# Splitting the first weight tile of five projection stages inside the stage in front of each

## The chip, the cores and the metric

One core of a Trainium2 chip runs the whole kernel in one launch. The metric is the device time of that core in microseconds (us), lower is better. The engines are TensorE (PE, with its weight loads shown as PEld), VectorE (DVE), ScalarE (ACT), GpSimd (POOL) and SyncE (SP), which issues nearly all DMA transfers.

## The reference

A first block (one layer) and a second block (two layers) work on 512 tokens of 2048 features; the second block also carries 256 context tokens. All of it is fp32.

```python
# first block
proj = rmsnorm(x) @ w_in                       # 2048 x 5120
y_s = s5_scan(u_s, ...); y_s = gelu(y_s)
y_s = y_s * sigmoid(y_s @ w_glu + b_glu) * silu(g_s)
y_d = diff_attention(q, k, v, ...) * silu(g_d)
y_x = memory_attention(q_x, rmsnorm(mem) @ w_mem_kv) * silu(g_x)
x = x + rmsnorm(concat([y_s, y_d, y_x]) @ w_out)
# second block, for l in 0, 1
h = rmsnorm_2(x) * (1 + scale) + shift         # from silu(c) @ ada_w[l]
q, k, v, up, uf, g = split_proj(h @ w_in[l])   # 2048 x 4608; context tokens too
att = latent_attention(rope(norm(q)), rope(norm(k)), v, kc, vc)
mixed = concat([att, multiscale_pool(up), fourier_mix(uf)])
x = x + gate * ((mixed * silu(g)) @ w_out[l])
# at the end rmsnorm_2(x)
```

## The kernel before

**How a weighted product is done.** Every large product is fp32 made of three fp32r products. The activations lie in SBUF as a high and a low part, `h_hi` and `h_lo`, features on partitions, tokens along the row (512, or 768 with context). A weight tile is 128 output columns by all 2048 inputs, 1 MB, and is used as 16 blocks of 128x128. It is loaded by SP into one of four slots of `raw`, ScalarE rounds it into `w_hi` (2 slots), VectorE writes `w_lo = raw - w_hi` (2 slots), and TensorE runs `w_hi*h_hi`, `w_hi*h_lo`, `w_lo*h_hi` over the 16 blocks into a PSUM bank. The counters (semaphores) are `raw_full[0..3]`, `hi_done`, `lo_done` and `w_used`. ScalarE may write `w_hi` of tile n when TensorE is through tile n-2 (`w_used.at(n - 1)`).

**The helper `linear`** (lines 220 to 412) runs one such product: a loop over tiles on each engine. On ScalarE tile n is split (line 319), then the result of tile n-1 is read out, then comes side work. VectorE does the same with line 348 for the split. TensorE waits for `lo_done.at(n + 1)` and runs lines 389 to 391. With `ahead` the two engines split the first tile of the following stage before the last result is read (lines 324 to 328 and 355 to 357), and with `primed` the four slots of `raw` were loaded by the stage in front.

**The stages in order.** `opening`, `ssm_and_conditions` (32 tiles of `w_in`, the state-space scan on VectorE and GpSimd, and the conditions from `ada_w`), a `linear` of 8 tiles of `w_mem` (the memory's keys and values, 256 tokens, with the preparation of the GLU as side work: class `GluPrepare`), `glu` (4 double tiles), `middle_attention` (16 units of differential and 16 of memory attention), `out_projection` with `w_out`, and then twice `projections(l)` (36 tiles), `layer_attention(l)` and `out_projection(w_out2, ...)` (16 tiles, through `linear`), and `final_norm`. Each stage is a block of the language: its engines start together once all five are through the stage in front, SP's last waits among them. Inside a block every engine runs its own list in the order written, and waits only on semaphores.

**Where the first split stands now.** In five stages it is the first instruction of ScalarE and of VectorE: the memory product (lines 319 and 348 of its first turn), `glu` (`split(0)`, lines 1272 and 1302), and the three calls of `out_projection` (lines 319 and 348). In the other stages with such products it is already done in the stage in front (`ahead`).

**What is around it.** At the end of `ssm_and_conditions` ScalarE copies the last result of the conditions (`ada_copy`, 957), the last projection result (`out_`, 947) and the last scan output (`y_copy`, 952); VectorE ends its scan at line 1051 and adds the conditions (1004). SP loads the four tiles of `w_mem` at line 893. In the memory product the side work of a turn is, on VectorE, lines 1177, 1182, 1186, 1188 and 1192, and on ScalarE lines 1164, 1166 and 1170; after the eighth turn three more turns of side work alone (`rest`) close the stage. In `middle_attention` ScalarE and VectorE run a loop over units g: read-out (1849), exponential (1823), gate (1842) and results on one, maximum (1909, 1911), weights (1925, 1927), gates (1941) and results (1946, 1953) on the other; each waits for the other in every unit. The last GpSimd instruction of the stage is line 1797. In `projections` the last turns (`kind == "mix"`, c = 0 to 9) also run the pooling and Fourier branches, and read-out of tile n is a tanh on ScalarE (2365) and a product on VectorE (`gate_out`, 2502). SP's turn c = 9 stores the last mixed rows (`store_mixed(3)`) and loads the first head (2320). `layer_attention` has SP load head 0's gate and mixed row, then call `prime` (line 414: four tiles of `w_out2`), and then load head 1's queries (1387).

```python
# before, linear, ScalarE: the split, then the read-out of the tile in front
for j in range(4):
    n = 4 * i + j
    act.wait_ge(raw_full[j].h, raw_full[j].at(16 * (i + 1)))
    act.wait_ge(w_used.h, w_used.at((n - 1) * per_slot))
    act.activation(w_hi[:, j % 2, 0:size], raw[:, j, 0:size], ACT.Copy).then_inc(hi_done.h, 1)
```

## Time and profile before

| | |
|---|---|
| median of 3 runs | 3012.83 us (3012.28 to 3015.34) |
| profiled execution | 3011.3 us |
| its span, first to last instruction | 3009.5 us |
| PE busy, share of span | 2825.9 us, 94% |
| DVE, ACT, POOL busy | 1517.9, 987.8, 503.3 us |
| mean granted TensorE clock | 0.973 of full speed |

```profile
PE   7899999988769999999999999899989999989897
PEld 5666665667447868888888877688878877867785
DVE  6587887867563552125533436423253385546334
ACT  4444444434353333122211126411142232226321
POOL 2544445424341030000000002100010000002000
PEclk9999999999789999999999999999999999999998
```

Each column is a fortieth of the span (75 us), each digit the busy share in tenths, and PEclk the granted TensorE clock in tenths. TensorE is nearly always busy; the columns with 6 to 8 are the attention stages and the ends of stages. The memory product, `glu`, `middle_attention` and the first `out_projection` lie in columns 9 to 14, the attention of layer 0 in columns 24 to 26, that of layer 1 in columns 36 and 37.

### The profile page before, as it was taken

The page shows a single profiled execution, that of the slowest core. Times are in us where ns is not written, and L with a number is a line of the kernel's source. Part 1 is how long each engine was busy: PE and PEld are TensorE (multiplying, and loading weights), DVE is VectorE, ACT ScalarE, POOL GpSimd, SP SyncE. Part 2 cuts the span into 40 slices and gives each one's busy share as a digit, 9 for nine tenths or more (in the row PEclk, how much of TensorE's full clock was granted, in tenths as well). Part 3 has the DMA queues.
Part 4 walks back from the last instruction along what each step waited for, and adds up shares of the span by engine and source line. Part 5 has one row for each costly group of instructions (what it writes and reads, how often), then busy time and mean ns, then how long its engine had stood idle before and what let it go on. Part 6 is the DMA issues. An engine that isn't in the chain of part 4 may idle for free. (4 is left out here: it accounts for less than half of the span.)

```text
span 3009.5 us, 36233 instructions
## 1 busy us (share of the span) xinstructions
PE 2825.9 (94%) x14018; PEld 2228.0 (74%) x14018; DVE 1517.9 (50%) x2057; ACT 987.8 (33%) x1708; POOL 503.3 (17%) x607
## 2 busy tenths in 40 slices
PE   7899999988769999999999999899989999989897
PEld 5666665667447868888888877688878877867785
DVE  6587887867563552125533436423253385546334
ACT  4444444434353333122211126411142232226321
POOL 2544445424341030000000002100010000002000
PEclk9999999999789999999999999999999999999998
DMA  5577787765213242233333341322313444441421
GB/s 189 183 306 304 286 313 290 282 248 175 101 57 126 86 180 83 78 110 134 117 108 131 121 159 64 116 78 96 119 49 107 143 168 147 154 163 60 161 98 56
DMA packets 111687, 447.20 MB, mean 149 GB/s; under 512 B 11440, under 2 KB 19760, under 8 KB 76208
## 3 DMA queue, kind: packets, MB, share of 16 engines
q1 hardware_dynamic: 111536, 445.16, 40.7%
q8 instruction: 98, 1.61, 0.2%
q14 instruction: 53, 0.43, 0.0%
HBM read 375.25 MB, written 69.86 MB: 148 GB/s over the span
## 5 line engine op out<-in xcount | busy, mean ns | idle before, releaser
L2732 PE MATMUL ps<-h_hi,w_hi 128*128 128x512 f32 x1600 | 576.9, 361 | 0.0
L2733 PE MATMUL ps<-h_lo,w_hi 128*128 128x512 f32 x1600 | 565.1, 353 | 0.0
L2734 PE MATMUL ps<-h_hi,w_lo 128*128 128x512 f32 x1600 | 561.4, 351 | 0.0
L389 PE MATMUL ps<-h_hi,w_hi 128*128 128x512 f32 (+1 forms) x1152 | 413.1, 359 | 35.0 <-DVE w_lo L348 35.0
L390 PE MATMUL ps<-h_lo,w_hi 128*128 128x512 f32 (+1 forms) x1152 | 412.1, 358 | 0.0
L391 PE MATMUL ps<-h_hi,w_lo 128*128 128x512 f32 (+1 forms) x1152 | 410.0, 356 | 0.0
L2732 PEld LDWEIGHTS ps<-h_hi,w_hi 128*128 128x128 f32 x1600 | 301.9, 189 | 49.8 <-issue 6.2
L2733 PEld LDWEIGHTS ps<-h_lo,w_hi 128*128 128x128 f32 x1600 | 301.7, 189 | 46.5 <-issue 6.2
L2734 PEld LDWEIGHTS ps<-h_hi,w_lo 128*128 128x128 f32 x1600 | 300.8, 188 | 43.7
L2510 DVE TENSOR_TENSOR w_lo<-raw,w_hi 128x2048 fp32r<-128x2048 f32 x64 | 146.4, 2287 | 310.7 <-ACT w_hi L2413 310.6
L389 PEld LDWEIGHTS ps<-h_hi,w_hi 128*128 128x128 f32 x1152 | 220.0, 191 | 70.1 <-DVE w_lo L348 37.9
L391 PEld LDWEIGHTS ps<-h_hi,w_lo 128*128 128x128 f32 x1152 | 219.2, 190 | 31.9
L390 PEld LDWEIGHTS ps<-h_lo,w_hi 128*128 128x128 f32 x1152 | 219.8, 191 | 30.5
L2366 ACT ACTIVATE xw<-ps 128x512 f32<-128x512 f32 x88 | 42.2, 517 | 593.4 <-PE ps L2734 552.9
L1465 POOL TENSOR_TENSOR h_lo<-xw,h_hi 128x768 fp32r<-128x768 f32 (+1 forms) x16 | 25.4, 1588 | 1237.1 <-ACT h_hi L1513 1237.1
L1111 PE MATMUL ps<-h_hi,w_hi 128*128 128x512 f32 x512 | 203.5, 397 | 12.9 <-DVE w_lo L1020 6.9
L1112 PE MATMUL ps<-h_lo,w_hi 128*128 128x512 f32 x512 | 200.2, 391 | 0.0
L1113 PE MATMUL ps<-h_hi,w_lo 128*128 128x512 f32 x512 | 200.2, 391 | 0.0
L2092 ACT ACTIVATE wide<-xw 128x512 f32<-128x512 f32 (+3 forms) x48 | 33.8, 703 | 486.9 <-DVE stat L2116 373.8
L348 DVE TENSOR_TENSOR w_lo<-raw,w_hi 128x2048 fp32r<-128x2048 f32 x56 | 128.7, 2303 | 87.6 <-ACT w_hi L319 87.6
L2108 DVE SCALAR_TENSOR_TENSOR xw<-ps,mods,xw 128x512 f32 (+3 forms) x48 | 31.8, 662 | 258.9 <-PE ps L391 244.7
L1111 PEld LDWEIGHTS ps<-h_hi,w_hi 128*128 128x128 f32 x512 | 96.6, 189 | 55.7 <-DVE w_lo L1020 21.2
(385 smaller groups left out, 4729.5 us busy)
## 6 DMA issues: line engine op xcount, KB each, us to landing
raw<-w_in SPq DMA_DIRECT2D x112, 1024.0 KB, 5.2
raw<-ada_w SPq DMA_DIRECT2D x96, 1024.0 KB, 8.3
raw<-w_out SPq DMA_DIRECT2D x48, 1024.0 KB, 4.9
proj<-xw SPq DMA_DIRECT2D x60, 384.0 KB, 2.6
xw<-proj SPq DMA_DIRECT2D x72, 256.0 KB, 3.4
xw<-proj SPq DMA_DIRECT2D x46, 384.0 KB, 3.4
xw<-resid SPq DMA_DIRECT2D x8, 1536.0 KB, 11.7
proj<-wide SPq DMA_DIRECT2D x32, 256.0 KB, 10.8
```

The source lines that it names most:

```text
L348: dve.tensor_tensor(w_lo[:, j % 2, 0:size], raw[:, j, 0:size], w_hi[:, j % 2, 0:size].bitcast(F32), ALU.subtract).then_inc(lo_done.h, 1)
L389: pe.matmul(a_[q], wh, h_hi[:, h0 + k, lo:hi], start=k == 0, stop=False)
L390: pe.matmul(a_[q], wh, h_lo[:, h0 + k, lo:hi], start=False, stop=False)
L391: ins = pe.matmul(a_[q], wl, h_hi[:, h0 + k, lo:hi], start=False, stop=k == nk - 1)
L1111: pe.matmul(acc, wh, h_hi[:, k, 0:T], start=k == 0, stop=False)
L1112: pe.matmul(acc, wh, h_lo[:, k, 0:T], start=False, stop=False)
L1113: ins = pe.matmul(acc, wl, h_hi[:, k, 0:T], start=False, stop=k == KC - 1)
L2366: act.activation(stage[par][:, a:b], a_, ACT.Copy)
L2510: dve.tensor_tensor(w_lo[:, j % 2, :], raw[:, j, :], w_hi[:, j % 2, :].bitcast(F32), ALU.subtract).then_inc(lo_done.h, 1)
L2732: pe.matmul(a_[q], wh, h_hi[:, k, a:b], start=k == 0, stop=False)
L2733: pe.matmul(a_[q], wh, h_lo[:, k, a:b], start=False, stop=False)
L2734: ins = pe.matmul(a_[q], wl, h_hi[:, k, a:b], start=False, stop=k == KC - 1)
```

## The change

A counter `first_hi` is added, `linear` and `out_projection` get a flag `begun`, and `projections` gets `then`. In the five stages the first split is left out, and the same two instructions (or pieces of them) are put into the stage in front:

- memory product: at the end of `ssm_and_conditions`, on ScalarE between `ada_copy` and `out_`, on VectorE between the end of the scan and the last `conditions`;
- `glu`: at the end of the memory product, by its `ahead` (before the last read-out, and so before the three turns of `rest`);
- first `out_projection`: in `middle_attention`, on ScalarE as two halves of 128x1024 at the ends of units g = 24 and 26, on VectorE as four quarters of 128x512 at the ends of units 26 to 29;
- `out_projection` of both layers: at the end of `projections(l)`, before the read-out of its last tile. SP loads the first tile of `w_out2` there (turn c = 9, before `store_mixed(3)`), and `layer_attention` loads only the other three. The function `prime` is gone.

```diff
@@ linear
+                            if not (begun and first(i) and j == 0):
+                                act.wait_ge(raw_full[j].h, raw_full[j].at(16 * (i + 1)))
+                                act.wait_ge(w_used.h, w_used.at((n - 1) * per_slot))
+                                act.activation(w_hi[:, j % 2, 0:size], raw[:, j, 0:size], ACT.Copy).then_inc(hi_done.h, 1)
...
+                            if not (begun and first(i) and j == 0):
+                                dve.wait_ge(hi_done.h, hi_done.at(n + 1))
+                                dve.tensor_tensor(w_lo[:, j % 2, 0:size], raw[:, j, 0:size],
+                                                  w_hi[:, j % 2, 0:size].bitcast(F32), ALU.subtract).then_inc(lo_done.h, 1)
@@ ssm_and_conditions
                     ada_copy(3 * LAYERS - 1)
+                    act.wait_ge(raw_full[0].h, raw_full[0].at(16 * (slots + 1)))
+                    act.wait_ge(w_used.h, w_used.at(slots - 1))
+                    act.activation(w_hi[:, 0, :], raw[:, 0, :], ACT.Copy).then_inc(hi_done.h, 1)
                     out_(slots - 1)
...
+                    dve.wait_ge(hi_done.h, hi_done.at(slots + 1))
+                    dve.tensor_tensor(w_lo[:, 0, :], raw[:, 0, :], w_hi[:, 0, :].bitcast(F32), ALU.subtract).then_inc(lo_done.h, 1)
                     conditions(3 * LAYERS - 1)
@@ glu, on ScalarE and on VectorE
-                    split(0)
@@ layer_attention
-                            prime(sp, then)
+                            for n in range(1, 4):
+                                sp.dma_start(raw[:, n, :], then(n)).then_inc(raw_full[n].h, 16)
@@ middle_attention
+                        if g in (D_UNITS + 8, D_UNITS + 10):
+                            c0 = (g - D_UNITS - 8) * T
+                            act.wait_ge(raw_full[0].h, raw_full[0].at(16))
+                            act.activation(w_hi[:, 0, c0:c0 + 2 * T], raw[:, 0, c0:c0 + 2 * T], ACT.Copy).then_inc(hi_done.h if c0 else first_hi.h, 1)
...
+                        if D_UNITS + 10 <= g < D_UNITS + 14:
+                            q = g - D_UNITS - 10
+                            w_ = slice(q * T, (q + 1) * T)
+                            dve.wait_ge(*((hi_done.h, hi_done.at(1)) if q > 1 else (first_hi.h, first_hi.at(1))))
+                            ins = dve.tensor_tensor(w_lo[:, 0, w_], raw[:, 0, w_], w_hi[:, 0, w_].bitcast(F32), ALU.subtract)
+                            if q == 3:
+                                ins.then_inc(lo_done.h, 1)
@@ projections
+                                sp.wait_ge(hi_done.h, hi_done.at(IN2 - 3))
+                                sp.wait_ge(lo_done.h, lo_done.at(IN2 - 3))
+                                sp.dma_start(raw[:, 0, :], then(0)).then_inc(raw_full[0].h, 16)
                                 store_mixed(3)
...
+                    act.wait_ge(raw_full[0].h, raw_full[0].at(4 * IN2 + 16 + late))
+                    act.wait_ge(w_used.h, w_used.at(IN2 - 1))
+                    act.activation(w_hi[:, 0, :], raw[:, 0, :], ACT.Copy).then_inc(hi_done.h, 1)
                     read_out(IN2 - 1, (IN2 - 1) % 2, before)
...
+                    dve.wait_ge(hi_done.h, hi_done.at(IN2 + 1))
+                    dve.tensor_tensor(w_lo[:, 0, :], raw[:, 0, :], w_hi[:, 0, :].bitcast(F32), ALU.subtract).then_inc(lo_done.h, 1)
                     gate_out(IN2 - 1)
@@ the calls
         linear(2, lambda n: row(w_mem, n), KC, 0, [(T, W)], store=lambda n: row(mkv, n), primed=True, side=prep,
-               then=lambda n: w_glu[n])
+               begun=True, ahead=True, then=lambda n: w_glu[n])
-        out_projection(w_out, 0, [(0, T)], None, then=first_layer, side=ctx_side)
+        out_projection(w_out, 0, [(0, T)], None, begun=True, then=first_layer, side=ctx_side)
-            projections(l)
+            projections(l, lambda n: row(w_out2, n + 16 * l))
```

## Rows read from the trace of the kernel before

**Rows 1.** Waits of PE, whole span: us in total, times, longest us
```profile
PE ps L389 <- DVE w_lo L348: 35.0, 10, 6.9
```

**Rows 2.** Timeline, start of the memory product: start us, us, instruction [idle before <-releaser]
```profile
646.64 0.66 PE L1078 MATMUL ps<-ident_sb,wide 128*128 128x128 f32 x4
654.21 0.58 PE L389 MATMUL ps<-h_hi,w_hi 128*128 128x256 f32 x1 [6.92 <-DVE w_lo L348]
...
649.93 3.71 ACT L319 ACTIVATE w_hi<-raw 128x2048 fp32r<-128x2048 f32 x2 [2.57 <-PEq L852]
...
664.37 0.63 ACT L1164 ACTIVATE xw<-xw 128x512 f32<-128x512 f32 x1
...
654.93 0.75 DVE L1177 SCALAR_TENSOR_TENSOR xw<-xw,cv 128x512 f32<-128x512 f32 x1 [0.78 <-DMA xw<-proj]
...
659.25 0.68 DVE L1182 SCALAR_TENSOR_TENSOR xw<-xw 128x512 f32<-128x512 f32 x1
```

**Rows 3.** Timeline, ACT and DVE at the end of `ssm_and_conditions`
```profile
644.59 0.60 ACT L947 ACTIVATE wide<-ps 128x512 f32<-128x512 f32 x1 [10.60 <-PE ps L1113]
...
647.44 0.26 DVE L1004 TENSOR_TENSOR mods<-ps,cv 128x16 f32<-128x16 f32 x2 [2.69 <-PE ps L1078]
```

**Rows 4.** Timeline, ACT, DVE and PE from the memory product's end to `glu`
```profile
709.92 0.64 ACT L1170 ACTIVATE h_hi<-xw 128x512 fp32r<-128x512 f32 x1 [0.29 <-DVE xw L1186]
...
717.06 3.71 ACT L1272 ACTIVATE w_hi<-raw 128x2048 fp32r<-128x2048 f32 x2 [1.33 <-PEq L254]
...
715.42 1.28 DVE L1192 SCALAR_TENSOR_TENSOR h_lo<-xw,h_hi 128x512 fp32r<-128x512 f32 x2
...
721.35 0.80 PE L1326 MATMUL ps<-h_hi,w_hi 128*128 128x512 f32 x1 [8.11 <-DVE w_lo L1302]
```

**Rows 5.** Timeline, ACT and PE at the end of `middle_attention` and after
```profile
904.85 3.71 ACT L319 ACTIVATE w_hi<-raw 128x2048 fp32r<-128x2048 f32 x2 [1.17 <-PEq L1619]
...
909.14 0.80 PE L389 MATMUL ps<-h_hi,w_hi 128*128 128x512 f32 x1 [6.37 <-DVE w_lo L348]
...
911.01 0.63 PE L390 MATMUL ps<-h_lo,w_hi 128*128 128x512 f32 x1
911.44 0.63 PE L391 MATMUL ps<-h_hi,w_lo 128*128 128x512 f32 x1
```

**Rows 6.** Half a tile on ACT, in `projections`: busy us, mean ns | idle before
```profile
L2396 ACT ACTIVATE w_hi<-raw 128x1024 fp32r<-128x1024 f32 x1 | 1.0, 1043 | 0.0
```

**Rows 7.** Timeline, SP and PE: first of `layer_attention(1)` and `out_projection` of layer 0
```profile
2683.85 0.34 SPq L1398 DMA_DIRECT2D xw<-proj  x1
...
2684.05 4.40 PE L1415 MATMUL ps<-xw 128*128 128x512 f32 x8 [2.43 <-PEq L2228]
...
1925.47 3.51 SPq L2128 DMA_DIRECT2D xw<-resid  x4
...
1929.72 0.79 PE L389 MATMUL ps<-h_hi,w_hi 128*128 128x512 f32 x1 [6.45 <-DVE w_lo L348]
```

**Rows 8.** Timeline, PE and DVE in `out_projection` of layer 1
```profile
2809.47 0.80 PE L389 MATMUL ps<-h_hi,w_hi 128*128 128x512 f32 x1 [6.46 <-DVE w_lo L348]
...
2826.97 2.29 DVE L348 TENSOR_TENSOR w_lo<-raw,w_hi 128x2048 fp32r<-128x2048 f32 x1 [1.38 <-ACT w_hi L319]
2833.47 0.75 DVE L2108 SCALAR_TENSOR_TENSOR xw<-ps,mods,xw 128x512 f32<-128x512 f32 x1 [4.20 <-PE ps L391]
...
2844.35 0.75 DVE L2108 SCALAR_TENSOR_TENSOR xw<-ps,mods,xw 128x512 f32<-128x512 f32 x1 [5.10 <-PE ps L391]
```

**Rows 9.** Timeline, PE in `layer_attention(1)`, head 1's first scores
```profile
2700.43 2.93 PE L1415 MATMUL ps<-xw,wide 128*128 128x512 f32 x4 [6.14 <-DMA wide<-proj]
```

**Rows 10.** Windows of 2 us: PE, PEld, DVE, ACT, POOL busy (x), PEclk, DMA share, GB/s
```profile
1924.00:1926.00 2.00, 0.00 (x0) 0.00 (x0) 0.00 (x0) 0.82 (x2) 0.72 (x1) 1.00 0.00 0
...
2684.00:2686.00 2.00, 1.95 (x3) 0.95 (x4) 0.00 (x0) 0.00 (x0) 0.00 (x0) 0.50 0.75 228
...
2694.00:2696.00 2.00, 0.29 (x3) 0.05 (x1) 1.80 (x4) 0.88 (x2) 0.00 (x0) 1.00 0.99 418
```

More of the change, by code:

```diff
@@ L221, in linear @@
                    stage_at=0, beside=None, keep=None, primed=False,
-                   side=None, then=None, ahead=False):
+                   side=None, then=None, ahead=False, begun=False):
             nslot = 4 * iters
@@ L408, in linear @@
                 acc_free.base += nslot * per_slot
-        def prime(sp, wslot):
-            for n in range(4):
-                sp.dma_start(raw[:, n, :], wslot(n)).then_inc(raw_full[n].h, 16)
         z_at = [wide[:, 4 * T + q * SSM_TILES:4 * T + (q + 1) * SSM_TILES] for q in range(3)]
@@ L1303, in split @@
                                           ALU.subtract).then_inc(lo_done.h, 1)
-                    split(0)
                     for b in range(8):
@@ L2078, in end, with out_projection @@
                 ctx_root.base += 1
-        def out_projection(weights, base, segs, gate_layer, then=None, side=None):
+        def out_projection(weights, base, segs, gate_layer, then=None, side=None, begun=False):
             a0, a1 = segs[0][0], segs[-1][1]
@@ L2135, in out_projection @@
             linear(4, lambda n: row(weights, n + base), KC, 0, segs, act_out=act_out, vec_out=vec_out,
-                   beside=load_context if gate_layer is None else reload, primed=True, then=then, ahead=then is not None, side=side,
+                   beside=load_context if gate_layer is None else reload, primed=True, begun=begun, then=then, ahead=then is not None, side=side,
                    keep=(lambda n: (row(resid, n), xrow(n)(0, W))) if keeps else None)
@@ L2146, in out_projection, with projections @@
                 s.base += v
-        def projections(l):
+        def projections(l, then):
             both, lat = [(0, T), (T, W)], [(0, T)]
@@ L2864, in program @@
             last = l == LAYERS - 1
-            projections(l)
+            projections(l, lambda n: row(w_out2, n + 16 * l))
             layer_attention(l, lambda n: row(w_out2, n + 16 * l))
-            out_projection(w_out2, 16 * l, [(0, T)] if last else both, l, then=None if last else lambda n: row(w_in2, n + IN2))
+            out_projection(w_out2, 16 * l, [(0, T)] if last else both, l, begun=True, then=None if last else lambda n: row(w_in2, n + IN2))
         final_norm()
```

9 lines of the change are left out of this document (2 added, 7 removed).

## The prediction

> **What bounds the kernel now.** I read the page first: PE is busy for 94% of the span, so time is won only where PE stands still or where a stage is not bound by PE. Then the waits of PE: lines 389 and 1326, the first products of the five stages, stand in front: 35.0 us of line 389 for a `w_lo` from VectorE, and 8.1 us ahead of `glu` [rows 1, 4]. Then I read the timeline of each engine at the five starts, and asked in each stage whether an earlier PE start reaches its end. Five gaps of 6.4 to 8.1 us make about 34 us; the others of line 389 are inside the memory product. Each gap has two parts: the way from the last product of the old block to the start of the new one, which stays, and the split (ScalarE 1.9 us, then VectorE 2.3), which the change moves.
>
> Where PE would start without the split: `layer_attention` has no split, and its first product comes 0.20 us after SP's first instruction (2684.05 against 2683.85) [rows 7]. I take block start plus 0.2 us everywhere.
>
> **Memory product.** The block starts at 649.9, PE at 654.21; without the split it starts at 650.1, 4.1 us sooner [rows 2]. VectorE gains nothing: its first side step (line 1177) waits for a load until 654.93, so line 1182 of turn 1 stays at 659.25 and is over at 659.9. What is late next is ScalarE: it reads tile 0 out once PE is through it, loads a table, and runs line 1164 at 664.37, long after its input was ready. From there the stage goes by a chain of ScalarE and VectorE with a period of 7.5 us, not by PE. With tile 0 done 4.1 us sooner, line 1164 comes at 660.3, still behind 659.9, so the chain and the end of the stage move by 4.1 us. A shorter slow phase of PE adds at most 0.4.
>
> What it costs in front: ScalarE was idle for 10.6 us ahead of its copy at 644.59, and VectorE for 2.7 us ahead of 647.44 [rows 3]. A 1.9 us split fits the first; one of 2.3 us, from the scan's end at 644.74, the second (over at 647.05). Were the cover gone, the first would cost 1.9 and the second 2.3. Cost nothing: **-4.1**.
>
> **glu.** Here the moved split lands in the stage's tail. ScalarE is through its last step of turn 7 (709.92) at 710.5, splits until 712.4, and VectorE until 714.7, ahead of the three turns of side work that now begin at 711.0 [rows 4]. These seven steps, 0.6 us apart, and the two waits for ScalarE among them, end at 716.70 now and at 719.5 then: I laid them out one by one, and the wait for ScalarE's tanh takes up part of the delay. So the block starts 2.8 us late (719.8 for 717.0) and PE at 720.0 instead of 721.35. That is 1.35 us won of 4.15. Bounds: nothing won if the whole 4.2 us is on the path; 4.15 if it hides. The eight products of `glu` then run without a gap, so the gain lasts: **-1.35**.
>
> **First out_projection.** The block starts at 904.85 and PE at 909.14 [rows 5]; 905.1 would be 4.05 sooner. Against it stand two ScalarE halves of 1.04 us [rows 6] and four VectorE quarters; a 128x512 step takes 0.68 [rows 2]. In these units ScalarE and VectorE wait for each other. The first half follows the high part of a result at the end of unit 24; it pushes the exponential of unit 27 and the gate by 0.5 us, the second half the exponential of unit 29 by another 0.8. Quarters 1 to 3 start while VectorE waits some 0.6 us for an exponential and fit; the fourth comes in front of the last weights and costs 0.6. Sum 1.9. Bounds: 0 if all hides, 2 x 1.04 + 4 x 0.68 = 4.8 if nothing does. I take 1.9, by the order of the units. Then PE runs through: 4.05 - 1.9, **-2.15** (between -4.05 and +0.75).
>
> **out_projection of the two layers.** In front the split hides: tile 34's result is read about 16 us (layer 0) or 11 us (layer 1) ahead of tile 35's, and both engines are idle between. SP's extra load goes out ahead of `store_mixed(3)`, whose `hi_done` and `lo_done` were passed by tile 32; behind it in SP's queue are two stores and three loads with 20 us to spare. Layer 0: block start 1925.47, PE at 1925.67 instead of 1929.72 [rows 7]: **-4.05**; the next splits have 6 us of slack. Layer 1: 2805.42 instead of 2809.47, but here something is late next. VectorE's split of tile 2 runs from 2826.97 to 2829.26, held by the result of tile 0, which waits for the reload of `resid`; that does not move. Tile 1 ended shortly before 2833.47 [rows 8] and would end at 2829.2. PE waits about 0.15 us: **-3.9**, and no more than that whatever PE does sooner.
>
> **layer_attention(1).** PE stands still for 6.14 us until 2700.43 for head 1's queries [rows 9]. SP issues that load behind the four tiles of `w_out2`, and in this stretch the DMA moves 418 GB/s [rows 10]. One tile less in front of it is 1.05 MB / 418 GB/s = 2.5 us. What is late next: the weights of unit 3, done at 2697.9, about when the load would land. **-2.5**, between 0 (if another transfer fills the place) and -3. In layer 0 head 1 begins after six units, and no such wait shows: 0.
>
> **Sum.** 4.1 + 1.35 + 2.15 + 4.05 + 3.9 + 2.5 = 18.05 us. The profiled execution (3011.3 us, 1.8 of it outside the span) becomes 2993.25. It is 1.5 below the median; off the median, 3012.83 - 18.05 = 2994.8 us.
>
> **The clock of TensorE.** Ahead of every start PE runs for 3 to 5 us at half clock (1.2 GHz): products are 0.43 us apart, against 10.88 / 48 = 0.23 in a tile at full clock [rows 5, 8]. I leave this as it is. At the start of layer 0's out_projection the granted clock was still 1.00 in the window in which PE would now start, 1924 to 1926; but after a gap just as short (2.43 us) the window 2684 to 2686 shows 0.50 [rows 7, 10]. If the full clock holds there, 1.6 us more come off in layer 0; in layer 1 the split of tile 2 takes it away. The Trainium skill ("TensorE: Matmul & The Clock Gate", section "Why this matters for your kernels") advises to keep the pauses between bursts of matmuls short, lest the clock fall back; by that rule the shorter pauses would hold the clock. Row 2684.05 speaks against it here.
>
> **Rivals.**
> - The clock holds: -19.7, 2993.1 us. For it the 1.00 at 1924, against it the 0.50 at 2684. 12%.
> - The moved splits are on the path of the stages in front (glu 0, first out_projection +0.75 instead of -2.15): 18.05 - 1.35 - 2.9 = 13.8, 2999.0 us. For it: both tails are chains of two engines that wait for each other. Against it the idle times that I laid out. 14%.
> - The same, and neither the memory product nor the attention gains, since another load sets their pace: 13.8 - 4.1 - 2.5 = 7.2, 3005.6 us. Against it ScalarE's 4.4 us of slack at 664.37 and the single DMA wait. 8%.
> - The change does nothing at the starts, as PE waits for something else there (`h_lo`, a bank, the reload): only the costs in front stay, some 2 us and the attention's gain against them: 3012 us, no change. Nothing waits so in the rows, since no other releaser is near. 4%.
> - Slower: the clock. If after the new, short pauses PE stays at half clock for longer than the 3 to 5 us of now, each product costs 0.2 us more, at the five starts and in layer 1's attention. It decides from 18.05 / 0.2 = 90 products; 120, 24 a stage, give 24 us and 3012.83 - 18.05 + 24 = 3018.8 us. For it: the clock does fall after pauses of 2.4 us. Against it: no start shows more than some 25 slow products, and those are in the numbers already. 3%.
> - My forecast, 2994.8 us, with terms within 2 us of their size: 59%.
>
> **How the numbers follow.** About 0.2%, 6 us, is what a measurement of this kernel tells from no change: below 3006.8 is faster, above 3018.9 slower. Faster: 59 + 12 + 14 and most of the 8%, some 0.91. Same 0.06, slower 0.03. The range reaches from the clock rival less 3 us (the terms at their upper bounds: glu 1.4 more, the out_projection 1.9 more) to beyond the third case's neighbour: 2989.5 to 3002.5. It leaves out the cases at 3005.6 and above, some 15%.
>
> **What would show it.** Right: the first products of the five stages come 0.2 us after the block's start, with a PEq or no releaser; the gaps are 2.8 us (memory product), 6.8 (glu), 2.4 to 4.3 (the three others). ScalarE's line 1164 comes 10.3 us after the memory product's block start instead of 14.4. The memory product's block is 1.3 us shorter, since its tail grows by 2.8. The differential and memory attention is 1.9 us longer between 887 and the next block. Head 1's wait in layer 1 is 3.6 us instead of 6.1. PE waits some 0.15 us ahead of tile 2 in the last out_projection. Wrong: a gap of over 5 us at an out_projection, a longer distance between the blocks of `ssm_and_conditions` and the memory product, a PE wait inside `glu`, or more slow products per start than now.

## The result

| | kernel before | changed kernel |
|---|---|---|
| median of the runs | 3015.34 us (3012.28 to 3021.37, 5 runs) | 2997.36 us (2995.03 to 3001.04, 5 runs) |
| profiled execution | 3011.3 us, span 3009.5 | 2996.14 us, span 2994.3 |
| mean granted clock of TensorE | 0.973 | 0.976 |

The ratio is 0.9935, 95% interval 0.9921 to 0.995: 18.0 us faster by the medians, 15.2 by the two profiled executions. In a second series (the first experiment) it was 0.9931 (0.9918 to 0.9943).

In the page of the changed kernel the busy times are those of before. What changed is the list of PE's waits (columns: us in total, times, longest). Line 393 is line 389 of before, and its wait for VectorE has fallen from 35.0 us, longest 6.9 [rows 1], to 10.3, longest 1.5. The start gaps now stand under PEq, PE's sequencer:

```profile
PE ps L393 <- DVE w_lo L352: 10.3, 8, 1.5
...
PE ps L1329 <- PEq L256: 6.7, 1, 6.7
...
PE ps L393 <- PEq L1383: 4.6, 2, 2.3
...
PE ps L1420 <- DMA wide<-proj: 4.2, 1, 4.2
```

The timeline (start us, us, instruction, idle before) of the five starts, SP's first instruction of the block where it has one and PE's first product, answers to [rows 2, 4, 5, 7, 8]:

```profile
652.55 0.34 SPq L1153 DMA_DIRECT2D xw<-ys  x1
...
652.68 0.36 PE L393 MATMUL ps<-h_hi,w_hi 128*128 128x256 f32 x1 [2.74 <-PEq L851]
...
717.84 0.33 SPq L1232 DMA_DIRECT2D wide<-pos  x1
...
718.03 0.77 PE L1329 MATMUL ps<-h_hi,w_hi 128*128 128x512 f32 x1 [6.73 <-PEq L256]
...
905.59 1.50 SPq L2149 DMA_DIRECT2D xw<-ctx_in  x3
...
905.67 0.77 PE L393 MATMUL ps<-h_hi,w_hi 128*128 128x512 f32 x1 [2.19 <-PEq L1624]
...
1919.59 0.47 PE L393 MATMUL ps<-h_hi,w_hi 128*128 128x512 f32 x1 [2.28 <-PEq L1383]
...
2793.00 4.02 SPq L2145 DMA_DIRECT2D xw<-resid  x4
...
2793.07 0.47 PE L393 MATMUL ps<-h_hi,w_hi 128*128 128x512 f32 x1 [2.28 <-PEq L1383]
```

PE starts 0.07 to 0.2 us after its block everywhere, instead of 4.25 to 4.36. So each start gained 4.2 us. Where that went is read from the lengths of the stages, from SP's first instruction to that of the next block (for the output projections, to the next stage's first product). Here are the lengths in us, with the experiments that are told below; a dash means that this part of the change is undone there, a star that its place is altered.

| stage | before | changed | again | undo_mid | undo_mem | undo_glu | load only | mid only |
|---|---|---|---|---|---|---|---|---|
| memory product | 67.1 | 65.3 | 66.4 | 66.8 | 69.1 - | 62.5 - | 66.7 | 66.7 |
| glu | 58.8 | 54.9 | 55.8 | 54.9 | 54.8 | 59.5 - | 60.1 | 60.1 |
| middle attention | 129.1 | 132.8 | 133.9 | 129.5 - | 132.7 | 133.2 | 131.3 | 134.1 |
| first out_projection | 183.9 | 180.2 | 180.1 | 183.9 | 180.1 | 180.1 | 186.1 | 180.1 |
| layer_attention(0) | 141.9 | 139.1 | 139.0 | 142.0 | 139.0 | 139.1 | 142.0 | 140.1 |
| out_projection, layer 0 | 277.5 | 273.4 | 273.4 | 273.4 | 273.4 | 273.4 | 277.5 | 278.5 |
| layer_attention(1) | 121.4 | 119.1 | 121.1 | 120.8 | 119.2 | 118.7 | 120.4 | 122.7 |
| out_projection, layer 1 | 182.5 | 179.6 | 181.3 | 178.7 | 179.7 | 179.8 | 183.0 | 182.6 |

In the six other kernels the rows that matter read: middle attention 134.0* (gap_mid), 135.3 (hold_loads), 129.2 (layers_only), 132.7* (quarters_mid), 133.8 (first_quarter), 132.8* (best, the last one below); last out_projection 179.3, 180.4*, 179.8, 179.5, 178.0* and 176.4*. In layers_only the middle attention is that of before.

In the pair of the first two columns the eight stages are 17.8 us shorter, and the stages ahead of them 2.6 us longer, which gives the 15.2 us of the profiled executions. One trace is one execution. The executions of one kernel spread by 6 us (the changed kernel) to 19 us (early_load_only, 3007.45 to 3026.05), so differences below 2 us in one stage are not read from one pair of traces but from how all of them group.

### The profile page after: what moved, and what is told of

Its sections match the earlier page's. It is cut to its first block and busy times, and to the rows that moved or that the text cites. A ratio compares the mean times of both kernels' runs of the same rounds, so it can differ in the third digit from the quotient of the medians.

```text
span 2994.3 us, 36239 instructions
## 1 busy us (share of the span) xinstructions
PE 2827.3 (94%) x14018; PEld 2227.6 (74%) x14018; DVE 1518.5 (51%) x2060; ACT 988.2 (33%) x1709; POOL 506.1 (17%) x607
## 5 line engine op out<-in xcount | busy, mean ns | idle before, releaser
L393 PE MATMUL ps<-h_hi,w_hi 128*128 128x512 f32 (+1 forms) x1152 | 412.6, 358 | 19.8 <-DVE w_lo L352 10.3
L2758 PEld LDWEIGHTS ps<-h_hi,w_hi 128*128 128x128 f32 x1600 | 301.9, 189 | 49.6 <-issue 6.2
L2534 DVE TENSOR_TENSOR w_lo<-raw,w_hi 128x2048 fp32r<-128x2048 f32 x64 | 146.4, 2288 | 311.7 <-ACT w_hi L2434 311.7
L393 PEld LDWEIGHTS ps<-h_hi,w_hi 128*128 128x128 f32 x1152 | 219.6, 191 | 55.3 <-DVE w_lo L352 12.2
L352 DVE TENSOR_TENSOR w_lo<-raw,w_hi 128x2048 fp32r<-128x2048 f32 x52 | 119.9, 2305 | 79.0 <-ACT w_hi L322 79.0
L919 POOL TENSOR_TENSOR xw<-xw 128x32 f32<-128x32 f32 (+3 forms) x128 | 97.6, 763 | 254.5 <-ACT xw L975 254.5
```

The lines of the kernel that those rows point to most:

```text
L352: dve.tensor_tensor(w_lo[:, j % 2, 0:size], raw[:, j, 0:size], w_hi[:, j % 2, 0:size].bitcast(F32), ALU.subtract).then_inc(lo_done.h, 1)
L393: pe.matmul(a_[q], wh, h_hi[:, h0 + k, lo:hi], start=k == 0, stop=False)
L919: pool.tensor_tensor(er[:, m:2 * m], gt[0][:, 0:m], gt[1][:, 0:m], ALU.subtract).then_inc(st.step(), 1)
L2534: dve.tensor_tensor(w_lo[:, j % 2, :], raw[:, j, :], w_hi[:, j % 2, :].bitcast(F32), ALU.subtract).then_inc(lo_done.h, 1)
L2758: pe.matmul(a_[q], wh, h_hi[:, k, a:b], start=k == 0, stop=False)
```

## Experiments

**1. The changed kernel again.** No edit.

> The changed kernel once more, unaltered. It separates what the change does from what varies between profiled executions. Theory (the edits explain the steps): PE-start gaps of 0.2 us at the four `linear` starts and glu, the middle attention block again 3 to 4 us longer than before, the first scores wait of layer 1 about 4.2 us, the resid reload wait of about 1.3 us ahead of tile 2 of the last output projection. Theory of phase: three things of the first trace have no edit behind them, the state-space stage that was 2.6 us longer, layer_attention(0) that was 3.0 us shorter, and the clock that rose again 3.0 to 3.4 us after each output projection's start; if they are only phase of the clock and of the loads they come out otherwise here, by 1 us or more each; if the edits make them, they repeat within 0.5 us. Time 2994 to 3001 us.

Measured 2998.51 us against 3018.47, ratio 0.9931 (0.9918 to 0.9943). The starts, the longer middle attention (+4.8), the shorter layer_attention(0) (139.0) and the longer state-space stage (521.0 us from its first product; 522.4 in the first trace, 518.4 before) repeat. What doesn't: the clock. In the last output projection of the first trace it was 0.61 in the first 4 us of the block; here it stayed at 1.00 for the block's first 24 us. PE was through tile 1 earlier and so waited longer ahead of tile 2 (2.92 us instead of 1.28). The stage was 1.6 us longer, not shorter: behind that wait the clock fell (0.50 from 2824 to 2826, the last line below). hold_loads shows the same (1.00 at the start, a wait of 1.99 us, then 0.50 from 2818.5 to 2820.5, and 180.4 us), while in undo_mid the clock stayed at 1.00 through a wait of 2.01 us and behind it, and the stage took 178.7 us. The windows of the block's first 4 us (busy us (count) of PE, PEld, DVE, ACT, POOL; granted clock; DMA share; GB/s), in the first trace and in this one:

```profile
2793.00:2797.00 4.00, 3.92 (x11) 3.15 (x12) 2.10 (x1) 1.87 (x1) 0.00 (x0) 0.61 0.71 204
```

```profile
2797.80:2801.80 4.00, 3.89 (x17) 3.27 (x18) 2.06 (x1) 1.91 (x1) 0.00 (x0) 1.00 0.70 209
...
2824.00:2826.00 2.00, 2.00 (x7) 1.52 (x6) 0.69 (x1) 2.00 (x2) 0.00 (x0) 0.50 0.93 262
```

**2. Undo one part.** undo_mid: the copies of line 1894, the subtractions of line 2012, and `begun` of the first out_projection are gone.

> The changed kernel without the part in the middle attention block: its two half copies and four quarter subtractions are gone and the first output projection splits its own first tile again. Theory (the pieces lengthen the middle block by what they delay on its path): the block goes back from 133 to 129.1 us (-3.7), the first output projection starts its products 4.2 us after its block and is 3.8 us longer; total within 1 us of the changed kernel, 2996 to 2998. Rival (the 3.7 us was clock phase, and the pieces cost the 1.9 us of the forecast): the block goes back by 1.9 us only or less, and the kernel is 2 us or more slower than the changed one (2998.5 to 3000).

Measured 3001.34 us, 0.9944 (0.993 to 0.9958); against the changed kernel's 0.9931 that is within the interval. Middle attention is 129.5 us, so the pieces cost 3.4 to 4.5 us and not 1.9 (from unit 26 on 22.2 and 22.5 us with them, 18.8 without), and the first out_projection gains 3.8: this part wins nothing where it stands. But layer_attention(0) was 142.0 again, which neither side had expected.

undo_mem, the split at the end of the state-space stage gone:

> The changed kernel without the part in the state-space stage: no split at its end, the memory product splits its own first tile. Theory (the split at the end of the state-space stage is hidden and the extra 2.6 us upstream of it were the run's own): first product of the memory product 4.3 us after its block instead of 0.2, the block some 1.8 us longer, and the state-space stage ends within 1 us of where it ended with the split; the kernel is 2 to 4 us slower than the changed one, 2998.5 to 3001. Rival (the split in front lengthens the state-space stage by 2.6 us): the stage ends 2 to 3 us earlier, and the kernel loses 1 us at most or gains.

Measured 3002.94 us, 0.9948 (0.9934 to 0.9961). The gap is back (PE 4.3 us after its block) and the block is 3.4 us longer than its mean of 65.7 with both halves. The state-space stage was 520.4 us. That alone would not settle whether the split lengthens it, since kernels without the split show from 518.3 (mid_only) to 523.6 (layers_only) and kernels with it from 519.6 to 524.6. The last stretch does: from the issue of `w_mem`'s load to the block's end it is 16.63 us before and in undo_mem, 16.62 in the changed kernel and 16.64 in its repeat. The split is hidden there. Four kernels, one of them without it, have 19.5 to 21.0 us in that stretch, and nothing in their edits reaches it.

undo_glu, `ahead` of the memory product and `begun` of glu gone:

> The changed kernel without the part in the memory product: glu splits its own first tile again. Theory (a gain at the start of glu less what the split costs at the end of the memory product): the memory product's block shorter by 2.0 us, 64.2 us instead of 65.3 to 66.8, glu's first product 4.4 us after its block instead of 0.2 and that block 3.5 us longer, 58.5 us; in all 1.5 us slower than the changed kernel. Rival (the tail costs as much as the start gains): both blocks together no longer than the 120.3 to 122.2 us of the changed kernel.

Measured 2999.15 us, 0.9945 (0.9929 to 0.9962). The two blocks take 122.0 us against 120.2, and 120.8 on average for the changed kernel's order: about 1.2 us, where the forecast had 1.35, made of 4.4 won at glu's start and 3.3 lost in the memory product's tail. The net is inside the spread of one trace, since the eight kernels with both halves show 119.9 to 122.2 us. Clearer is undo_mem, which has only this part: 124.0 us for the two blocks, against 125.9 to 126.9 in the four kernels with neither. With undo_mem and undo_glu there are all four states of the memory product: 66.9 with neither half (mean of four), 62.5 with only its own start made early (-4.4), 69.1 with only glu's split in its tail (+2.2), 65.7 with both.

**3. Do one part.** early_load_only, on the kernel before:

```
+   sp.dma_start(raw[:, 0, :], then(0)) ...   # in projections, c == 9
-   prime(sp, then)
+   for n in range(1, 4): sp.dma_start(raw[:, n, :], then(n)) ...
```

> The kernel before with one thing of the change: tile 0 of w_out2 is loaded inside the projections stage, with that stage's own slot released, and layer_attention issues only tiles 1 to 3. No split is moved. Theory (the wait of the first scores of a head is for its load behind w_out2 tiles on one queue): layer 1's wait ahead of its second head falls from 6.14 to 4.2 us and that block is 2 us shorter; layer_attention(0) unchanged (141.6 us block to block), the gaps at the stage starts remain 4 us; in all 2 us faster than before, 3009 to 3011. Rival (the 3.0 us that layer_attention(0) was shorter comes from this load too): both attention blocks shorter, in all 5 us, 3006 to 3008. In the last output projection the reload of resid lands as before, 18.3 us after the block's start, with no PE wait for it.

Measured 3018.7 us, 0.9998 (0.9985 to 1.001): no change that can be told, where 2 us were expected. The wait went as the theory has it, from 6.14 us [rows 9] to 3.92:

```profile
2705.32 2.93 PE L1416 MATMUL ps<-xw,wide 128*128 128x512 f32 x4 [3.92 <-DMA wide<-proj]
```

mid_only is the mirror of undo_mid: only the middle block's pieces, on the kernel before.

> Of the change only the part in the middle attention block: two half copies and four quarter subtractions in its last units, and the first output projection begins without its own first split. Theory: the block 3 to 5 us longer (132.5 to 134.5 instead of 129.1), the first output projection 3.8 us shorter (180.1 instead of 183.9), so nothing by itself; but layer_attention(0) 139.0 us instead of 142.0, as in the six kernels whose first output projection has no gap, though nothing in that block, in the projections ahead of it or in its loads is changed. Rival (the other parts of the change make that block shorter): 142.0 us. In all 0 to 3 us faster than before by the theory, 0 to 1 slower by the rival.

Measured 3014.91 us, 0.9995 (0.9986 to 1.0005): nothing by itself, as expected. Its wait for head 1's queries is 6.81 us, so with and without the early load there are two groups: 6.14 and 6.81 without, 3.52 to 4.49 in the twelve traces with it, and layer_attention(1) 121.4 and 122.7 us against 119.5 on average (118.6 to 121.1). layer_attention(0) took 140.1 us, neither of the two values expected.

layers_only: the early load and the split of `w_out2`'s first tile, nothing else.

> Of the change only the parts of the two layers: the early load and the split of w_out2's first tile at the end of each projections stage. Memory product, glu and first output projection as before. Theory (the parts add up): both layer output projections start their products 0.1 us after their blocks, the first of them is 4.0 us shorter (273.4 instead of 277.4), the last 1.2 to 3.8 us shorter with a wait of 1 to 3 us ahead of tile 2, layer_attention(1) 0.5 to 2.2 us shorter; layer_attention(0) 142.0 us, since the first output projection has its gap; in all 6 to 10 us faster than before, a ratio of 0.9967 to 0.998. Rival for layer_attention(0) (it is the parts of the layers that make it shorter): 139.0 us.

Measured 3007.35 us, 0.9969 (0.9956 to 0.9983), 10 us of 20. The out_projections took 273.4 and 179.8 us, layer_attention(1) 119.1.

**4. Another place for the middle split.** gap_mid puts a whole copy into unit 4 and a whole subtraction into unit 8, where both engines were idle (5.91 us ahead of 836.84 on VectorE):

```
+   if g == 4: act.activation(w_hi[:, 0, :], raw[:, 0, :], ACT.Copy)          # behind exp(g + 2)
+   if g == 8: dve.tensor_tensor(w_lo[:, 0, :], raw[:, 0, :], w_hi[:, 0, :])  # ahead of rope(3, 0)
```

> The changed kernel with the middle attention block's split in another place: one whole copy by ScalarE behind the exponentials of unit 4, where it then sat idle for 6.84 us, and one whole subtraction by VectorE in unit 8, ahead of a wait of 5.91 us for the rotated keys. The block's last units have no split any more. Theory (the pieces cost what they delay in the last units): the block is as long as with no split at all, 129 to 131 us instead of 132.8 to 134.0, and the first output projection still starts its products 0.1 us after its block; 3 us faster than the changed kernel. Rival (GpSimd's products beside it make the subtraction, or are made, longer, and the rotation is on the path): 131 us or more. On layer_attention(0): it was 139.0 us in the three kernels whose first output projection starts without its gap and 142.0 us in the three that have the gap; by that reading it is 139.0 here, and if the pieces in the middle block made it, 142.0.

Measured 3001.97 us, 0.9953 (0.9936 to 0.997), no better, and the block took 134.0 us. The rival was right. From the peak of unit 26 (line 1917 at 891.95) to the end of the block it was 19.4 us, near the 18.9 of before and not the 22.2 of the changed kernel, so the tail was healed; the loss had moved. The timeline, VectorE and GpSimd:

```profile
835.86 3.35 DVE L1985 TENSOR_TENSOR w_lo<-raw,w_hi 128x2048 fp32r<-128x2048 f32 x1
...
837.02 3.31 POOL L1777 TENSOR_TENSOR xw<-xw,wide 128x512 f32<-128x512 f32 x1
840.41 1.26 POOL L1779 TENSOR_TENSOR xw<-xw,wide 128x512 f32<-128x512 f32 x1
```

The subtraction that takes 2.3 us alone took 3.35, and the GpSimd product beside it, 1.26 us in the rows around it, took 3.31. The numbers fit a lock that the one who comes first holds to its end: VectorE began at 835.86, while GpSimd's step of 835.80 ran until 837.06, and 1.2 us of that and 2.3 of its own make 3.5 against 3.35 measured; GpSimd's next began at 837.02 and had to wait until 839.21, and 2.19 and 1.26 make 3.45 against 3.31. The Trainium skill ("SBUF — State Buffer", section "SBUF: two separate sides") says this of VectorE steps with two inputs from SBUF, against GpSimd steps that read SBUF: they share a port pair, and the later one is blocked and not slowed. The trace agrees to 0.15 us, and the forecast should have used it. That product is in the chain to the rotated keys, for which VectorE and PE waited: the idle time was GpSimd's work, and it could not be used for a step that holds GpSimd up.

quarters_mid keeps the copy and puts four quarters where VectorE was idle for 0.6 to 1 us and GpSimd had nothing to do: the ends of units 5, 9 and 13, and ahead of the read-out in unit 15.

> The changed kernel with the middle attention block's split placed by the idle times of its first units: the whole copy by ScalarE in unit 4, as in gap_mid, but the subtraction in four quarters (some 0.68 us each) at the ends of units 5, 9 and 13 and ahead of the read-out in unit 15, where VectorE sat idle 0.98, 0.98, 0.9 and 0.59 us and GpSimd had nothing to do. Theory (in gap_mid one GpSimd product of 1.26 us lasted 3.31 us beside the whole subtraction, and that was the block's loss there; away from GpSimd a piece costs only what exceeds the idle time): the block takes 129 to 131.5 us, its last six units as long as with no split, and no GpSimd product of 128x512 lasts over 1.4 us in it; 3 us faster than the changed kernel. Rival (each piece costs its own length wherever it stands, since idle time just moves): 132 us or more.  layer_attention(0) 139.0 us by the reading that it follows the gap of the first output projection.

Measured 2994.12 us (2991.17 to 2996.39), 0.9922 (0.9904 to 0.9941), some 3 us under the changed kernel's ratio, within the interval. The quarters took 0.68 us:

```profile
821.33 0.68 DVE L1966 TENSOR_TENSOR w_lo<-raw,w_hi 128x512 fp32r<-128x512 f32 x1
...
842.54 0.68 DVE L1966 TENSOR_TENSOR w_lo<-raw,w_hi 128x512 fp32r<-128x512 f32 x1
```

The tail is healed (19.6 us from unit 26's peak, 883.39, to 902.97), but the block took 132.7 us, above the 131.5 expected and in the rival's range. Up to unit 26 the block's chain took 113.2 us here and again in best, 110.3 before, and the difference of 2.9 us is near the 2.7 of four quarters. Against that reading stands hold_loads, whose split is at the end: 113.1 us, with a granted clock that ran in the same way for the block's first 108 us, so the clock alone may make it. Against hold_loads (135.3) the block is 2.5 us shorter. What the quarters cost of their own is not settled. And layer_attention(0) was 141.9, though the first out_projection had no gap: the reading that it follows that gap falls.

**5. The wait ahead of tile 2.** The changed kernel waits there, in the last out_projection. First the suspicion that the loads of later tiles delay the reload of `resid`. hold_loads:

```
-   sp.wait_ge(lo_done.h, lo_done.at(n - 3))
+   sp.wait_ge(lo_done.h, lo_done.at(n - 1))   # in out_projections with begun; hi_done likewise
```

> The changed kernel with the loads of tiles 4 to 15 in the output projections held back until tile n-1 is split (n-3 before), so that the 6 MB reload of resid has the queue alone after the first tiles. Theory (the reload, not the split, is what tile 2 of the last output projection waits for: the read-out of tile 0 needs resid and stands ahead of tile 2's subtraction on VectorE): the reload lands by 17 us after the block's start instead of 19.2, the wait of TensorE ahead of tile 2 (1.28 and 2.92 us in two traces of the changed kernel) is gone or under 0.3 us, and that stage takes 178.3 us or less instead of 179.6 and 181.3; no other stage changes. Rival (the loads of the later tiles don't compete with it; the 6 MB just take that long, and the earlier start of the products uncovers them): the wait stays between 1.0 and 3.0 us.

Measured 2998.95 us, 0.9944 (0.9927 to 0.9961). The theory falls. The timeline of DVE and PE in the changed kernel, then in hold_loads:

```profile
2812.15 0.75 DVE L2125 SCALAR_TENSOR_TENSOR xw<-ps,mods,xw 128x512 f32<-128x512 f32 x1 [14.95 <-DMA xw<-resid]
...
2817.99 0.50 PE L393 MATMUL ps<-h_hi,w_hi 128*128 128x512 f32 x1 [1.28 <-DVE w_lo L352]
```

```profile
2792.44 3.31 SPq L2146 DMA_DIRECT2D xw<-resid  x4
...
2810.69 0.75 DVE L2126 SCALAR_TENSOR_TENSOR xw<-ps,mods,xw 128x512 f32<-128x512 f32 x1 [14.05 <-DMA xw<-resid]
...
2816.54 0.50 PE L394 MATMUL ps<-h_hi,w_hi 128*128 128x512 f32 x1 [1.99 <-DVE w_lo L353]
```

Without any other load behind it the reload still landed 18.3 us after the block's start, as before (2823.48 after 2805.22). What goes with the landing is SP's own time for the four issues: 3.27, 3.31, 3.32 us where it landed at 18.3 (before, hold_loads, undo_mid), 4.02 and 4.07 where it landed at 19.2 (changed kernel and repeat).

first_quarter then takes away what is waited for, not a competitor: the read-outs of tiles 0 and 1 wait for the first of the four transfers only.

```
-   dve.wait_ge(resid_in.h, resid_in.at(64))
+   dve.wait_ge(resid_first.h, resid_first.at(16))
+   if n > 1: dve.wait_ge(resid_in.h, resid_in.at(48))
```

> The changed kernel with a semaphore of its own for the first of the four transfers of the reload of resid: the read-outs of tiles 0 and 1 wait for that quarter alone, that of tile 2 for all four. Theory (what keeps tile 2 of the last output projection waiting is that VectorE's read-out of tile 0 waits for all 6 MB, which land 18.3 or 19.2 us after the block's start with or without other loads beside them): the first read-out of that stage starts by 15 us instead of 18.3 to 19.2, TensorE's wait ahead of tile 2 (0.94 to 2.92 us in seven traces) is gone, the stage takes 178.2 us or less instead of 178.7 to 181.3. Rival (the four transfers share the queue and land together): the first quarter lands within 1.5 us of the last, and the wait stays over 0.9 us. No other stage changes.

Measured 2997.85 us, 0.9934 (0.9915 to 0.9953). Shown at its place, too small for the interval:

```profile
2808.59 0.75 DVE L2128 SCALAR_TENSOR_TENSOR xw<-ps,mods,xw 128x512 f32<-128x512 f32 x1 [8.68 <-PE ps L396]
```

The read-out comes 12.9 us after the block's start and waits for PE's product, no longer for the DMA; PE has no wait ahead of tile 2; the stage takes 178.0 us. With the full clock at the start and behind it, in the last kernel, it took 176.4.

**6. Both.** quarters_mid and first_quarter together.

> Both: the quarters of quarters_mid in the middle attention block, and the first quarter of the reload with its own semaphore as in first_quarter. Theory (the two gains are at different places and add): last six units of the middle block as with no split, 19.0 to 19.7 us from the peak of unit 26 to the block's end instead of 22.2 to 22.5; no wait of TensorE ahead of tile 2 in the last output projection, that stage 178.0 us; a ratio to the kernel before of 0.991 to 0.9925, 3 to 6 us less than the changed kernel. Rival (a shifted phase of the clock takes it back elsewhere: layer_attention(0) 142 instead of 139 us): 0.993.

Measured 2994.15 us (2988.54 to 2997.54, 6 runs) against 3019.54, ratio 0.9916 (0.9897 to 0.9935). It is the lowest ratio of the study and 25 us under the kernel before on the same chip; against the changed kernel's 0.9931 and 0.9935 the intervals still touch. Both gains are at their places (middle attention from unit 26 on 19.6 us, last out_projection 176.4), and layer_attention(0) was 141.9 us again, as the rival said, though the ratio is the theory's.

## Why the prediction was right, and where not

Forecast: 18.05 us faster, 2994.8 us from the median of 3012.83. Measured: 18.0 us between the medians, 20.0 on the second chip; of the 2.6 us between 2994.8 and 2997.36, 2.5 are those by which the median of before moved when it had five runs. The agreement of the sum is better than that of its terms, and that much of it is luck: the middle attention cost 2 us more than forecast, the last out_projection gave 1 us less, and layer_attention(0), put at 0, gave 3 us. (The range's lower end, 2989.5, would by the terms that it names be 2989.8.) Here the terms are, beside the mean over all traces in which the part is present, less the mean of those in which it isn't:

| step | forecast | measured |
|---|---|---|
| memory product, start less tail | -1.3 | -1.2 (eight traces against four) |
| glu | -4.15 | -4.4 |
| middle attention, split in its last units | +1.9 | +3.9 (+3.3 of it from unit 26 on) |
| first out_projection | -4.05 | -4.4 (-3.8 without early_load_only's 186.1) |
| out_projection, layer 0 | -4.05 | -4.4 (-4.1 without mid_only's 278.5) |
| layer_attention(1) | -2.5 | -2.6 (twelve traces against two) |
| out_projection, layer 1 | -3.9 | -2.9 (without first_quarter and best) |
| layer_attention(0) | 0 | -2.9 in the pair of traces, not explained by an edit |

**Starts.** Right. PE came 0.07 to 0.2 us after SP's first instruction at all five, and the gaps were 2.74, 6.73, 2.19, 2.28 and 2.28 us; the last three lie a little below the 2.4 to 4.3 written. One of the prediction's signs of being wrong did appear, a longer distance between the blocks of `ssm_and_conditions` and the memory product (522.4 us for 518.4). It doesn't count against it, since from the load of `w_mem` on, where the moved split lies, the distance is unchanged (experiment 2).

**Memory product.** Right in kind and size. ScalarE's first step, line 1164 of before, came 9.9 us after the block instead of 10.3 and 14.4 [rows 2], and VectorE is what it now waits for:

```profile
662.42 0.63 ACT L1169 ACTIVATE xw<-xw 128x512 f32<-128x512 f32 x1 [0.55 <-DVE xw L1187]
```

Alone, the start is worth 4.4 us (forecast 4.1), and the tail costs 2.2 us without that start and 3.3 with it (forecast 2.8).

**First out_projection.** The step that failed. "Quarters 1 to 3 start while VectorE waits some 0.6 us for an exponential and fit", the prediction said, and "the second half the exponential of unit 29 by another 0.8". The timeline of the changed kernel, ACT and DVE:

```profile
885.00 1.04 ACT L1894 ACTIVATE w_hi<-raw 128x1024 fp32r<-128x1024 f32 x1
885.95 0.37 ACT L1854 ACTIVATE xw<-ps 128x256 f32<-128x256 f32 x1
...
891.27 1.05 ACT L1894 ACTIVATE w_hi<-raw 128x1024 fp32r<-128x1024 f32 x1
892.22 0.38 ACT L1854 ACTIVATE xw<-ps 128x256 f32<-128x256 f32 x1
...
889.90 0.68 DVE L2012 TENSOR_TENSOR w_lo<-raw,w_hi 128x512 fp32r<-128x512 f32 x1
890.62 0.16 DVE L1935 RECIPROCAL wide<-wide 128x1 f32<-128x1 f32 x1
...
891.96 1.31 DVE L2012 TENSOR_TENSOR w_lo<-raw,w_hi 128x512 fp32r<-128x512 f32 x1
893.20 0.15 DVE L1935 RECIPROCAL wide<-wide 128x1 f32<-128x1 f32 x1
```

Each half of ScalarE stands ahead of line 1854, the read-out of a transposed tile, for which PE waits next: 1.13 us at 886.46 and 1.40 at 892.74, against 0.18 and 0.46 at the same places before (888.18 and 894.12). I had followed the exponentials and not this read-out. And a quarter took 1.31 us instead of 0.68, behind a GpSimd subtraction that began at 891.46 and held it up for the difference. PE before, then in the changed kernel:

```profile
894.12 0.41 PE L1692 MATMUL ps<-ident_sb,xw 128*128 128x128 f32 x2 [0.46 <-ACT xw L1849]
...
901.36 1.41 PE L1714 MATMUL ps<-xw 128*128 128x256 f32 x4 [0.47 <-ACT xw L1849]
```

```profile
892.74 0.66 PE L1697 MATMUL ps<-ident_sb,xw 128*128 128x128 f32 x2 [1.40 <-ACT xw L1854]
...
900.24 0.69 PE L1697 MATMUL ps<-ident_sb,xw 128*128 128x128 f32 x2 [2.04 <-DVE xw L1937]
901.40 2.07 PE L1719 MATMUL ps<-xw 128*128 128x256 f32 x4 [0.47 <-ACT xw L1854]
```

Counted from the peak of unit 26 (886.04 and 883.38), the first of these rows is 1.3 us later than before, the last four products start 2.7 us later, and the block ends 3.4 us later. So ScalarE's two halves cost the 1.3 us that the prediction gave them, by another wait. The stretch between the two rows, in which three of the quarters stand (891.96, 894.44, 898.71) and PE waits 2.04 us for VectorE's weights, costs 1.4 us and not 0.6: "fit" is what failed. The last 0.7 us is the clock, at which the prediction put nothing: the granted clock was 0.50 for the block's last 6 us instead of less than 3, and the same four products took 2.07 us instead of 1.41. The other six traces with these pieces show the same: 8.6 to 8.7 us between the two rows (7.2 before) and 2.07 or 2.08 us for the four products.

The bound of 4.8 us in the prediction was the right end to look at: the pieces cost 3.9 us on average and the start wins 3.8, so the part wins nothing, as mid_only and undo_mid both show. The rival in which moved splits are on the path was right for this stage and wrong for glu (124.0 us against 125.9 to 126.9, experiment 2).

**Last out_projection.** The named limit, the reload, was the right one, its size was off by 1 us. The prediction let PE wait 0.15 us, with the reload fixed and tile 1 ending at +23.9. The reload landed up to 1.1 us later (19.4 us after the block's start in layers_only), and with the clock up PE was done up to 1.8 us sooner: 0.94 to 2.92 us of waiting in nine traces. first_quarter shows the wait to be that one semaphore's.

**layer_attention(1).** Right: wait 4.22 instead of 6.14, forecast 3.6, and block -2.6 on average:

```profile
2688.63 2.93 PE L1420 MATMUL ps<-xw,wide 128*128 128x512 f32 x4 [4.22 <-DMA wide<-proj]
```

**The clock.** I left it as it was. At the two layers' starts the clock was still full for PE's first 0.6 to 0.8 us (products 0.31 and 0.24 us apart at 1919.59 and 2793.38) and then fell, so about half a microsecond was saved. In the repeat, undo_mid and hold_loads it didn't fall at the start of layer 1's, and the wait for the reload took most or all of the gain, as the prediction had it for that layer; at layer 0's it fell in every trace. (Where the prediction has the half clock "ahead of every start", its rows show it from the start on: the products 0.43 us apart at 911.01 are among the new block's first.) The slower rival had nothing for it. On pauses, the Trainium skill ("TensorE: Matmul & The Clock Gate", section "Why this matters for your kernels") advises to keep those between bursts short. The pause ahead of the last output projection was 2.28 us in the changed kernel and in its repeat, and the clock of the block's first 4 us was 0.61 in the one and 1.00 in the other: here a short pause permits the full clock and does not secure it. Over the runs the mean granted clock rose from 0.972 (17 of before) to 0.975 (5 of the changed kernel); most of that is, by estimate, the missing gaps themselves: the windows of the five gaps before stand at 0.50 to 0.67, and taking 21 us at some 0.57 out of 3010 raises the mean by 0.003.

**Left open: layer_attention(0).** SP issues one load fewer in this block, but undo_mid and layers_only have that too and took 142.0 us, and no compute instruction changed. Its 2.9 us stand in the windows after the block's start (columns as in experiment 1). The kernel before, then the changed one:

```profile
1783.50:1786.50 3.00, 2.78 (x5) 1.61 (x6) 0.00 (x0) 0.00 (x0) 0.00 (x0) 0.50 0.98 323
1786.50:1789.50 3.00, 3.00 (x8) 1.69 (x7) 1.40 (x3) 0.99 (x2) 0.00 (x0) 0.50 1.01 395
1789.50:1792.50 3.00, 1.27 (x10) 0.90 (x9) 2.56 (x7) 1.69 (x3) 0.00 (x0) 0.99 1.02 429
```

```profile
1780.50:1783.50 3.00, 2.85 (x5) 1.67 (x6) 0.00 (x0) 0.00 (x0) 0.00 (x0) 0.50 1.00 327
1783.50:1786.50 3.00, 2.75 (x13) 1.53 (x11) 2.60 (x6) 1.37 (x3) 0.00 (x0) 0.99 0.99 398
1786.50:1789.50 3.00, 1.28 (x9) 0.91 (x8) 1.58 (x5) 1.97 (x4) 0.00 (x0) 1.00 1.01 423
```

The granted clock came back 3 us sooner, and near the block's end a second low stretch was shorter. Over the 14 traces the block took 139.0 to 139.2 us seven times, 141.9 to 142.0 six times, 140.1 once (mid_only). It repeated in the one kernel with two traces and was at first in step with the gap of the first out_projection, 900 us earlier; quarters_mid and best broke that. Windows of 1 us separate the two groups without an exception. In the last us ahead of the block the granted clock was 0.59 to 0.71 in the six long ones and 0.79 to 0.95 in the eight others, so it had fallen earlier in a pause of PE that is 3.03 us in the kernel before and 3.04 in the changed one; and in the six it was still 0.50 between 5 and 6 us into the block, in the eight others 1.00. The kernel before, then the changed one:

```profile
1782.53:1783.53 1.00, 0.00 (x0) 0.00 (x0) 0.11 (x1) 0.00 (x0) 0.00 (x0) 0.59 0.05 18
1788.53:1789.53 1.00, 1.00 (x5) 0.79 (x4) 0.32 (x1) 0.30 (x2) 0.00 (x0) 0.50 0.95 401
```

```profile
1779.47:1780.47 1.00, 0.00 (x0) 0.00 (x0) 0.10 (x1) 0.00 (x0) 0.00 (x0) 0.83 0.05 22
1785.47:1786.47 1.00, 0.75 (x3) 0.30 (x2) 0.93 (x4) 0.63 (x3) 0.00 (x0) 1.00 0.99 410
```

What sets the moment of the fall stays open. It counts: the terms above sum to 16 us (15 without the two stray traces), the medians gave 18 to 20, and this block's 3 us, which seven of the ten traces without that gap and none of the four with it have, would be most of the rest. That is arithmetic and not shown; against it, quarters_mid and best had the long block and the lowest ratios.

## What to carry to other kernels

Splitting a stage's first weight tile in the stage in front wins the whole start where the stage in front ends with both engines idle (here 4.4 and 4.1 us, and 2.9 where a late reload took the rest), but where it ends in a chain of two engines that wait for each other, every piece costs what it delays, above all ahead of a read-out that TensorE waits for next; place the pieces by idle times, and ask of each idle time which engine is working in it. When a start moves forward by 4 us, list what the old start covered: the last output projection's reload was late only once TensorE was early. Wait for the transfer that the step needs, not for all that share its semaphore.

## What the hardware showed that I had not expected

- VectorE and GpSimd hold each other up with tensor-tensor steps from SBUF: a GpSimd 128x512 product took 3.31 us instead of 1.26 beside a VectorE 128x2048 subtraction, which took 3.35 instead of 2.3; a VectorE 128x512 step took 1.31 instead of 0.68 beside a GpSimd one.
- Four issues of the same 1.5 MB transfers take SP from 3.27 to 4.25 us from execution to execution, and the data land later by about as much (18.3 to 19.4 us after the first issue).
- The same block, instruction for instruction, can be 3 us longer or shorter (139.0 in first_quarter, 141.9 in quarters_mid) with the moment at which the granted clock falls in the pause ahead of it (about 6.8 us at half clock, or about 3.4, by windows of 1 us), so a stage's length in one trace of each kernel is no evidence below that.
